# Hybrid diffusion trunk on one core: gated attention of the even mixer done in another order, its output products spread over four parts of the array

## The reference

```python
def even_mixer(a, ac, ...):
    hy, q, k, v, g, lf, lb = project(a)          # one input projection, gates lf/lb forward and backward
    oc_f, sc_f = gla_chunked(qc, kc, vc, lfc, s0)   # context first
    o_f, _ = gla_chunked(q, k, v, lf, sc_f)         # latent goes on from its state; the same backward
    y = concatenate([hyena(hy), gla_merge(o_f + o_b, g)]) @ w_out

def gla_chunked(q, k, v, log_a, s0):             # chunks of 64 tokens, 4 heads, dk 64, dv 128
    att = where(mask, q_in @ k_in.T, 0)          # scores inside a chunk
    ds = k_st.T @ v                              # what a chunk adds to the state
    s_next = decay * s + ds                      # scan over the chunks
    o = att @ v + q_in @ s_before                # the outputs

def gla_merge(o, g):  return rms_norm(o, norm_g) * silu(g)
def hyena(hy):        # short convolution, z = part0 * part1, then irfft(rfft(z) * k_hat) + skip * z, times part2
```

## Time and profile before

| | us |
|---|---|
| median of 3 runs | 1786.51 (1784.61 to 1789.89) |
| profiled execution | 1783.22, of which span 1781.4 |
| PE busy | 1722.3 (97%) |
| DVE busy | 1155.9 (65%) |
| ACT busy | 679.9 (38%) |
| DMA, mean | 140 GB/s |

### The profile page before, as it was taken

The page is one execution under the profiler, slowest core; times in us unless marked ns, Lnnn a source line. Parts: engine busy times, 40 slices in busy tenths (PEclk is TensorE's granted clock), DMA queues, the critical chain, the costliest instruction groups (busy, mean ns, idle before and its releaser), DMA issues.

```text
span 1781.4 us, 24471 instructions
## 1 busy us (share of the span) xinstructions
PE 1722.3 (97%) x9690; PEld 1466.8 (82%) x9690; DVE 1155.9 (65%) x1777; ACT 679.9 (38%) x1021; POOL 72.8 (4%) x60
## 2 busy tenths in 40 slices
PE   6999999999999799999999999999999999999996
PEld 4788888889777689888888888888888886889996
DVE  4367949877484728678733366878466676665556
ACT  4452232226442315632222237322322373564443
POOL 1000000011000002000000020000000200100001
PEclk9999999999999969999999999999999999989998
DMA  9565546532332003455332233554565431145653
GB/s 340 197 197 177 164 164 215 188 98 85 104 116 77 1 1 119 166 187 188 118 98 92 82 135 116 192 175 144 167 219 175 136 107 44 59 143 163 203 161 103
DMA packets 81512, 250.08 MB, mean 140 GB/s; under 512 B 8740, under 2 KB 18117, under 8 KB 81270
## 3 DMA queue, kind: packets, MB, share of 16 engines
q1 hardware_dynamic: 79576, 245.46, 41.7%
q0 software_dynamic: 448, 1.57, 0.3%
q10 hardware_dynamic: 1374, 1.48, 0.2%
HBM read 247.43 MB, written 1.05 MB: 139 GB/s over the span
## 4 chain that ended last, share of the span: by engine, by line
PE 89%; DVE 5%; ACT 3%; issue 2%; DMA 0%; SPq 0%; ACTq 0%; DVEq 0%; PEldq 0%
PE bank L1678 26%; PE bank L1680 26%; PE bank L1679 26%; PE bank L1797 3%; PE bank L2107 1%; PE bank L2057 1%; DVE w_lo L1040 1%; PE bank L2204 1%; PE bank L1885 1%; ACT w_hi L727 1%; DMA raw<-in_dram 0%; ACT tmp_b L759 0%; PE bank L1722 0%; ACT a_hi L756 0%; PE bank L2195 0%
## 5 line engine op out<-in xcount | busy, mean ns | idle before, releaser
L1678 PE MATMUL bank<-a_hi,w_hi 128*128 128x512 f32 (+1 forms) x1576 | 572.2, 363 | 8.2 <-DVE w_lo L1040 5.0
L1679 PE MATMUL bank<-a_hi,w_lo 128*128 128x512 f32 (+1 forms) x1576 | 570.2, 362 | 0.0
L1680 PE MATMUL bank<-a_lo,w_hi 128*128 128x512 f32 (+1 forms) x1576 | 570.0, 362 | 0.0
L1040 DVE TENSOR_TENSOR w_lo<-raw,w_hi 128x1024 fp32r<-128x1024 f32 (+1 forms) x342 | 387.6, 1133 | 195.5 <-ACT w_hi L727 188.7
L727 ACT CAST w_hi<-raw 128x1024 fp32r<-128x1024 f32 (+1 forms) x342 | 324.3, 954 | 163.2 <-DMA raw<-in_dram 162.7
L1678 PEld LDWEIGHTS bank<-a_hi,w_hi 128*128 128x128 f32 x1576 | 298.1, 189 | 57.3 <-issue 7.7
L1680 PEld LDWEIGHTS bank<-a_lo,w_hi 128*128 128x128 f32 x1576 | 298.1, 189 | 45.4
L1679 PEld LDWEIGHTS bank<-a_hi,w_lo 128*128 128x128 f32 x1576 | 298.2, 189 | 45.1
L1058 DVE SCALAR_TENSOR_TENSOR acc<-ada,scol,acc 128x1024 f32<-128x1024 f32 x189 | 234.9, 1280 | 4.4 <-DMA ada<-in_dram 2.2
L1678 PE MATMUL bank<-h_hi,w_hi 128*128 128x512 f32 (+1 forms) x638 | 230.2, 361 | 0.0
L1680 PE MATMUL bank<-h_lo,w_hi 128*128 128x512 f32 (+1 forms) x638 | 229.8, 360 | 0.0
(11 more groups left out here) (273 smaller groups left out, 1787.3 us busy)
## 6 DMA issues: line engine op xcount, KB each, us to landing
raw<-in_dram SPq DMA_DIRECT2D x229, 512.0 KB, 3.6
ada<-in_dram SPq DMA_DIRECT2D x120, 512.0 KB, 3.9
raw<-in_dram SPq DMA_DIRECT2D x64, 384.0 KB, 3.1
raw<-in_dram SPq DMA_DIRECT2D x64, 320.0 KB, 2.9
first<-in_dram SPq DMA_DIRECT2D x32, 256.0 KB, 7.9
first<-in_dram SPq DMA_DIRECT2D x8, 512.0 KB, 6.3
hz<-in_dram SPq DMA_DIRECT2D x4, 512.0 KB, 7.7
window<-in_dram SPq DMA_DIRECT2D x1, 1024.0 KB, 11.5
```

What stands on the lines that cost most here:

```text
L1040: V.tensor_tensor(lo_of(n)[:, 0:cols], raw[:, n % RING, 0:cols], hi_of(n)[:, 0:cols].bitcast(F32), ALU.subtract).then_inc(s["lo_ready"], 1)
L1678: pe.matmul(dst, w_at(0), x_at(0), start=first, stop=False, skip_group_check=shared)
L1679: pe.matmul(dst, w_at(1), x_at(0), start=False, stop=False, skip_group_check=shared)
L1680: return pe.matmul(dst, w_at(0), x_at(1), start=False, stop=last, skip_group_check=shared)
```

## The change

The products are the same. PE's order becomes: scores right after the `e_hy` units; `e_g` 0; turn the keys; `e_g` 1; four chunk states; `e_g` 2; four chunk states; `e_g` 3; turn z; outputs of t = 2, 3; the eight forward transforms; outputs of t = 0, 1; inverse 0, 1; turn the outputs; inverse 2, 3; the first four `e_out` units, k-tiles 4 to 7 (gated attention) ahead of 0 to 3 (Hyena). `sum_mods(2)` and `take_mods(2)` move into the `e_hy` units. DVE masks and scans before the spectra, and puts the sums of squares between them. The outputs are issued in rounds: in each round one product to each of up to four parts (row half x column half) of the array. `ds_sb` and `state` become two tiles each, other tiles move to other addresses. The core of the diff (moved blocks that are only removed are cut):

```diff
+O_ORDER = (2, 3, 0, 1)
...
-    proj("e_g", GH, "g_read")
+    p.mark(("e_g", 0))
+    for h in range(GH):
+        u = p.unit("e_g", (h,), UCOL)
+        p.base[("e_g_job", h)] = p.job(("w_used", u), ("g_read", p.bump("g_read")))
+        if h in (1, 2):
+            for i in range(NCH // 2):
+                p.base[("ds_job", (h - 1) * NCH // 2 + i)] = p.job(("ds", p.bump("ds")), ("ds_read", p.bump("ds_read")))
...
-    jobs("ds", NCH, "ds_read")
...
-        ds = put("ds_sb", [P, NCH, 2, 2, P], at=X + 16 * K)
+        ds_two = [put(f"ds_sb{i}", [P, NLAT, 2, 2, P], at=X + (24 + 16 * i) * K) for i in range(2)]
-        state = put("state", [P, NCH, 2, 2, P], at=X + 40 * K)
+        state_two = [put(f"state{i}", [P, NLAT, 2, 2, P], at=X + (8 + 40 * i) * K) for i in range(2)]
-        yt = put("yt", [P, YC, T], at=X + 40 * K)
+        yt = put("yt", [P, YC, T], at=X)
...
-        osqr = put("osqr", [P, TC, GH * GDV], at=X + 8 * K)
-        o_sb = put("o_sb", [P, TC, GH * GDV], at=X + 16 * K)
+        osqr = put("osqr", [P, TC, GH * GDV], at=X + 24 * K)
+        o_sb = put("o_sb", [P, TC, GH * GDV], at=X + 40 * K)
...
-                    j = first_job("e_g") + h
+                    j = plan.base[("e_g_job", h)]
                     job_ready(act, j)
                     A.activation(gs[:, h, :], jbank(j)[:], ACT.Silu).then_inc(s["g_read"], 1)
+                    if h == 0:
+                        act.wait_ge(s["zf_ready"], YC)
+                        for t in range(TC):
+                            act.wait_ge(s["kst_turned"], t + 1)
+                            A.copy(kstt[:, t].rearrange("p a b c -> p (a b c)"), bank[4 + t][:]).then_inc(s["kst_read"], 1)
+                    elif h < 3:
+                        for at in range((h - 1) * NCH // 2, h * NCH // 2):
+                            j = plan.base[("ds_job", at)]
+                            job_ready(act, j)
+                            A.copy(ds_of(DS_ORDER[at]).rearrange("p a b c -> p (a b c)"), jbank(j)[:])\
+                                .then_inc(s["ds_read"], 1)
                 split_to(first_unit("e_out") + 4)
                 for t in range(TC):
                     j = first_job("z_turned") + t
                     job_ready(act, j)
                     A.copy(zt[:, t, :], jbank(j)[:]).then_inc(s["zt_read"], 1)
-                act.wait_ge(s["zf_ready"], YC)
-                for t in range(TC):
-                    act.wait_ge(s["kst_turned"], t + 1)
-                    A.copy(kstt[:, t].rearrange("p a b c -> p (a b c)"), bank[4 + t][:]).then_inc(s["kst_read"], 1)
-                for c in range(KC):
-                    keep(1, c)
+                act.wait_ge(s["state_ready"], NCH - 1)
+                for at, t in enumerate(O_ORDER):
+                    act.wait_ge(s["o_done"], at // 2 + 1)
+                    A.activation(osqr[:, t, :], bank[4 + t][:], ACT.Square).then_inc(s["o_sq"], 1)
+                    if at == 1:
+                        for c in range(KC):
+                            keep(1, c)
+                for h in range(GH):
+                    act.wait_ge(s["gla_out"], h + 1)
+                    A.copy(a_hi[:, YC + h, :], go[:, h, :]).then_inc(s["cat_hi"], 1)
                 act.wait_ge(s["idft"], YC)
                 for c in range(YC):
                     act.wait_ge(s["cat"], c + 1)
                     A.copy(a_hi[:, c, :], yt[:, c, :]).then_inc(s["cat_hi"], 1)
...
-                take_mods(2)
+                        if e == 9:
+                            take_mods(2)
+                split_to(first_unit("e_out"))
+                dve.wait_ge(s["gla_in"], 32)
+                lim = [bound[:, i].rearrange("p d (h c) -> p d h c", h=1).to_broadcast([P, 2, GH, GCH]) for i in range(2)]
+                for t in range(TC):
+                    dve.wait_ge(s["att"], t + 1)
+                    V.tensor_tensor(attm[:, t], bank[4 + t][:].rearrange("p (d h c) -> p d h c", d=2, h=GH), lim[0],
+                                    ALU.min).then_inc(s["att_read"], 1)
+                for t in range(TC):
+                    dve.wait_ge(s["att_read"], t + 1)
+                    V.tensor_tensor(attm[:, t], attm[:, t], lim[1], ALU.max).then_inc(s["att_kept"], 1)
+                for t in range(TC):
+                    dve.wait_ge(s["att_kept"], t + 1)
+                    V.tensor_tensor(attm[:, t, 0], attm[:, t, 0], attm[:, t, 1], ALU.add).then_inc(s["att_masked"], 1)
+
+                order = ([4, 5, 6, 7, 0, 1, 2, 3], [7, 6, 5, 4, 3, 2, 1, 0])
+                for step in range(NCH - 1):
+                    dve.wait_ge(s["ds_read"], (2, 4, 4, 8, 8, 8, 8)[step])
+                    if step:
+                        dve.wait_ge(s["state_ready"], step)
+                    for d in range(2):
+                        now, nxt = order[d][step], order[d][step + 1]
+                        for hp in range(2):
+                            if step == 0:
+                                ins = V.tensor_copy(state_of(nxt)[:, d, hp, :], ds_of(now)[:, d, hp, :])
+                            else:
+                                ins = V.scalar_tensor_tensor(state_of(nxt)[:, d, hp, :], state_of(now)[:, d, hp, :],
+                                                             dec[:, d, hp, now:now + 1], ds_of(now)[:, d, hp, :],
+                                                             ALU.mult, ALU.add)
+                    ins.then_inc(s["state_ready"], 1)
+                    if step == 2:
+                        split_to(first_unit("e_out") + 2)
...
+                def square_sums(at):
+
+                    t = O_ORDER[at]
+                    dve.wait_ge(s["o_sq"], at + 1)
+                    return V.tensor_reduce(stat[:, 0, t * GH:(t + 1) * GH],
+                                           osqr[:, t, :].rearrange("p (h c) -> p h c", h=GH), AX_X, ALU.add)
...
                 spectra(0)
                 spectra(1)
-
-                dve.wait_ge(s["gla_in"], 32)
-                for t in range(TC):
-                    dve.wait_ge(s["att"], t + 1)
...
+                square_sums(0)
+                square_sums(1)
                 spectra(2)
                 spectra(3)
-
-                for c in range(YC):
+                square_sums(2)
+                link(square_sums(3))
+                link(V.tensor_scalar(stat[:, 0, :], stat[:, 0, :], 1.0 / GDV, RMS_EPS, ALU.mult, ALU.add))
+                rsqrt(stat[:, 1, :], stat[:, 0, :], stat[:, 2, :])
+                for t in range(TC):
+                    r = stat[:, 1, t * GH:(t + 1) * GH].rearrange("p (h c) -> p h c", c=1)
+                    V.tensor_tensor(o_sb[:, t, :].rearrange("p (h c) -> p h c", h=GH),
+                                    bank[4 + t][:].rearrange("p (h c) -> p h c", h=GH),
+                                    r.to_broadcast([P, GH, GDV]), ALU.mult).then_inc(s["o_scaled"], 1)
...
+                def lower_cat(c, at, src):
+
+                    dve.wait_ge(s["cat_hi"], at + 1)
+                    V.tensor_tensor(a_lo[:, c, :], src, a_hi[:, c, :].bitcast(F32), ALU.subtract)\
+                        .then_inc(s["cat_ready"], 1)
+
+                hyena_out(0)
+                hyena_out(1)
                 for h in range(GH):
                     dve.wait_ge(s["o_turned"], h + 1)
                     dve.wait_ge(s["g_read"], h + 1)
                     V.scalar_tensor_tensor(go[:, h, :], bank[4 + h][:], pcol("gla_g"), gs[:, h, :],
                                            ALU.mult, ALU.mult).then_inc(s["gla_out"], 1)
                     if h >= 1:
...
+                        lower_cat(YC + h - 1, h - 1, go[:, h - 1, :])
+                lower_cat(KC - 1, GH - 1, go[:, GH - 1, :])
+                hyena_out(2)
+                hyena_out(3)
+                for c in range(YC):
+                    lower_cat(c, GH + c, yt[:, c, :])
...
+                    if e == 9:
+                        pe.wait_ge(s["v_read"], TC)
+                        sum_mods(2)
...
+                def gate_unit(h):
+
+                    bank_read(pe, plan.base[("e_g_job", h)])
+                    project(first_unit("e_g") + h, plan.base[("e_g_job", h)], T)
...
+                def gla_pair(ta, tb):
+
+                    for phase in range(2):
+                        if phase:
+                            pe.wait_ge(s["o_lower"], O_ORDER.index(ta) // 2 + 1)
+                        queues = []
+                        for t, top in ((ta, phase), (tb, 1 - phase)):
+                            rows = slice(top * GCH, (top + 1) * GCH)
+                            for b in range(2):
+                                cc = 2 * t + b
+                                cols = slice(cc * GCH, (cc + 1) * GCH)
+                                terms = []
+                                if b == top:
+                                    terms += [(h, attm[rows, t, 0, h, :], v[rows, t, h * GDV:(h + 1) * GDV])
+                                              for h in range(GH)]
```

(121 more changed lines are left out.)

116 lines of the change are left out of this document (6 added, 110 removed).

## The result

The changed kernel takes 1754.83 us in the median of four runs (1753.47 to 1759.34), the kernel before 1786.13: ratio 0.9826, 95% interval 0.9811 to 0.9841. Forecast were 1757.3 us and a range of 1752 to 1770. Measured again beside other kernels it took 1759.29 against 1787.52 (0.984, 0.9824 to 0.9856).

The account below looks back on a forecast made before the run. PE, busy 97%, was taken to bound the kernel through its gaps and slow stretches. Outputs 18.0, gaps 7.1, slow clock 2.8 and small gaps 1 checked the 29.2 us saving: 1786.5 to 1757.3 us, range 1752 to 1770.

Parts of the forecast that it names:

- The place: Gated-attention outputs in the even mixer: PE held first by DVE (spectra, masks, scan), then by its own way of issuing.
- Up to the first outputs: From 543.3 us, PE works 35.6 us without a wait, to 578.9; masks, scan and ACT's waits hidden.
- The outputs: Two pairs of gated-attention outputs at full clock: 3.7 and 4.2 us instead of 25.9.
- serial bound: Rival at the outputs: one quarter at a time, 107 ns per instruction, pairs 9.0 and 10.7 us, 1769.0 us; chance 0.06.
- From the transforms on: Start 582.6, DVE leads: last spectrum 19.1 us later, Hyena 3 bank read by 38.0, with a 3.0 us PE wait.
- The sum: First four `e_out` units end at 642.4 against 671.6 us: 29.2 us less.
- the clock that fell behind the 2.8 us wait: Rival: clock falls after the 3.0 us gap (1.4 us) or under quarter-array work; about 10 us in all, 1767; chance 0.10.
- check of terms: Mixer saving by terms: outputs 18.0, gaps 7.1, slow clock after two waits 2.8, 28 in all, and 1 for small gaps.
- lower clock: Slow clock after two waits: 1.4 us in the first inverses, the same assumed for k-tiles after the outputs; 2.8 us saved.
- small gaps that no row here names: Remainder of the mixer saving beyond the named terms: 1 us.
- Strict order: Rival at PE's outputs: products start in program order, 54 ns per instruction, pairs 4.7 and 5.6 us, 1759.5; chance 0.14.
- Draining at each change of row half: Rival at the outputs: alternating row halves costs 274 ns per instruction, pairs 22.3 and 26.7 us, 1798; chance 0.03.

Follow-up runs that it names:

- e5: Changed kernel with ten more unused 128x512 operations on DVE (7 us) between the second spectrum and the sums of squares; 1761.55 us.
- e1: Changed kernel with each pair's output products issued queue after queue instead of in rounds over the four quarters; 1768.12 us.
- e2: Kernel before, order kept, with only the outputs issued in rounds over four quarters in two pairs of t; 1768.7 us.
- e3: Changed kernel with rounds over the two column halves of one t, then the other, row halves not interleaved; 1760.3 us.
- e6: Changed kernel with the first pair of outputs behind the wait for zt instead of ahead of it; 1762.04 us.
- e7: Changed kernel with `e_out` units 0, 1 ahead of the banks of 2, 3, and half the odd mixer's value projection before the query rotations; 1753.23 us.

## Why the prediction was right

*The place.* PE in the mixer held first by DVE, then by its own way of issuing: e5 (for the part from the transforms on) bears out the one, e1, e2 and e3 the other.

*Up to the first outputs.* Forecast: turned z done at 578.9, everything else hidden. It was done at 579.2, and no wait of PE stands between 543 and that point. Masks, scan, mods and ACT's new waits cost nothing.

*The outputs.* Forecast 3.7 and 4.2 us, measured 3.5 and 3.9. The unknown was the rate with four quarters at work; 32 ns was read from the changes of row half in the chunk states, and it is 27 in the mean, a quarter of the 0.11 us that one quarter takes. With 27 and 54 ns and the same handover the sum gives 3.4 and 3.9. The bounds were well placed: queue after queue takes 15.4 us, less than the serial bound of 18.8, since queues overlap where one follows the other.

*From the transforms on.* Forecast start 582.6, last spectrum 19.1 us later, first `e_out` product 38.0 us later. Measured 582.68, 19.15 (601.83), 37.8 (620.48).

*The sum.* Forecast 29.2 us less in the stretch, measured 27.8. The 1.4 us are the clock that fell behind the 2.8 us wait (some 1.7, less the 0.2 by which the first `e_out` product came sooner than forecast); the text had it as a rival at 1.4, beside a sum at full clock. By the prediction's own check of terms: outputs 18.0 forecast, 18.5 measured; gaps 7.1 and 7.6, since the 0.9 us wait for `ds_sb` was there to be gained, most of the "1 for small gaps that no row here names"; lower clock 2.8 and 1.5 (1.4 in the first inverses of before, 1.8 behind its outputs, where the granted clock is 0.50 from 648 to 650 us and 0.62 to 652, less the new 1.7). That makes 27.6. The measured medians differ by 31.3 in one comparison, 3.5 more than the stretch gives, and by 28.2 in the other. The first median lies 2.5 us under the forecast although the stretch saved 1.4 less than forecast: the mechanism was right, and how close the number came is in part luck. What lies beyond the stretch fits the spread of the odd mixer, which the prediction treated as noise without naming its source.

*The rivals.* Strict order is ruled out by e3, which it would have left at the changed kernel's time, and by the starts: each product is one matmul of the program and two instructions in the trace, yet the first instructions of all four queues start (579.18 to 579.20) ahead of the second of the first queue, some 0.15 us later. That speaks against the rule of the Trainium skill ("TensorE: Matmul & The Clock Gate", Part 3) that products start in strict program order; before, too, products of a later queue start between those of an earlier one. Its other rule there, that a pack takes one matmul plus some nanoseconds per tile, is close: four starts within 0.02 us, and the next four 0.11 us on. Draining at each change of row half did not occur. The clock fell under the outputs in the three traces with a wait right ahead of them (before, e2, e6) and in none of the eight others, which have none there.

## What to carry to other kernels

When small products use a quarter of the array each, issue them in rounds over all four quarters; here that alone took 17 us out of 26. (The pairs are formed so that the long queues lie in diagonal quarters; no run tests that choice by itself.) Find the engine that paces each stretch, take from it what can stand under another engine's dense work, and look for the next wait in the list: the last gap of 2.8 us fell to swapping which units come first. Compare kernels by fixed events of their traces before comparing medians, if one stretch is known to vary.

## What the runs showed of the hardware

- A product of 64x64x128 in float32 is two instructions. In one quarter of the array they start 0.11 us apart at the full clock (five in a row from 599.71 to 600.25 in e1) and 0.21 us apart at the lower level (before). With four quarters at work four start within 0.02 us, and the next four 0.11 us on: 27 ns each in the mean (changed kernel).
- Quarter-array outputs ran at granted clock 1.00 where PE had worked without a wait ahead of them (8.6 us of them in e1), and lost it where a wait of 2.0 us (e6) or 3.0 us (before, e2) stood ahead.
- A wait of 2.0 us does not always do so: PE waits as long for `w_lo` near 498 us in most of these traces, and the full-width products behind it ran at 1.00 from 500 to 506 us in the kernel before and at 0.52 from 500 to 503 in e7.
- Full-width work after a wait of 2.8 us was at the lower clock too, for 3.4 us in the changed kernel and 6.8 in e6; after 3.6 us of wait for 6.8 us in e1 and 3.4 in e3. The length of the wait does not order these.
- In the odd mixer the clock fell early for 3.4 us or late for 6.8 us in two executions of the changed kernel, and that decides between 26.6 and 29.9 us. What there brings it down was not isolated.
